# Dropping the softmax division from a differential attention block: the sum's square enters the norm's epsilon

## Chip, cores and metric

The kernel runs on one core of one Trainium2 chip. The metric is the device time of one execution in microseconds. Before the change it is 756.2 us, the median of 3 runs (755.72 to 756.58).

## The reference

One transformer block over 512 rows of width 2048: an RMS norm, a projection to six groups of 1024 columns (q, k, v, gate of the attention, pool input, gate of the pool), differential attention with 8 heads, a pooling branch, and an output projection added to x. What matters here is the attention and the norm behind it:

```python
s = einsum(q, k) * scale                      # two maps (c = 0, 1) for each head
p = softmax(s, axis=-1)
a = p[:, :, 0] - lam * p[:, :, 1]
o = einsum(a, v)                              # 2 * 64 columns a head
o = o * rsqrt(mean(o * o) + EPS) * subln_w * (1.0 - lam_init)
```

The norm's mean runs over the 128 columns of a head. With E0 and E1 for the exponentials and S0, S1 for their sums over the keys, a = E0 / S0 - lam * E1 / S1.

## The kernel before, in words

All products of TensorE are made of three: each fp32 operand is split into a high part (`w_hi`, `h_hi`, `at_hi`, cast to fp32r) and a low part (`w_lo`, `h_lo`, `at_lo`, the rest), and high times high, low times high and high times low are added in PSUM. The work has four stages. First v is projected (32 half tiles), then k of the first round. Then come four rounds (`ROUNDS`), of two heads each. Last come seven passes of the output projection (`out_half`), a scheme of seven half-sized products that take the place of eight.

A round has 40 steps, `for m in range(8, 48)`, written out by hand on every engine. In step m TensorE multiplies one half tile of weights, 512 columns, for the groups Q, U, GA, GP and K (of the next round; in the last round the first halves of the output projection). ScalarE casts the half tile of step m + 3 (`split_high`, L705) and VectorE subtracts to get its low part (`split_low`, which is `split_rest`, L923). ScalarE's cast waits on `w_used`, until TensorE has freed the buffer; VectorE's subtraction waits for the cast. Between these stands all other work of the round, each piece tied to a step.

Attention is done in eight items a round, two heads by four blocks of 128 query rows. For item i, counted from 0:

- TensorE computes both score maps in step 22 + 2i.
- VectorE takes the row maxima in step 23 + 2i (L1075), ScalarE the two exponentials in step 24 + 2i with their row sums in `row_sum` (L801).
- In step 24 + 2i VectorE forms 1/S0 and 1/S1 (`row_inv`, L1089), `coef` = -lam * S0 / S1 (L1090) and `at_raw` = E0 + coef * E1 (L1094).
- In step 25 + 2i ScalarE multiplies `at_raw` by 1/S0 (L825), and VectorE transposes it in 32x32 blocks (L1085), behind a wait for that scaling.
- SyncE moves the blocks with four DMAs (L383). In step 28 + 2i ScalarE casts `at_hi` (L808) and GpSimd subtracts to get `at_lo` (L474).

A head's product with v is run by TensorE at the end of steps 35 and 43. Behind it: ScalarE squares (`head_out`, L723, in steps 39 and 44), VectorE adds the squares over the partitions (the fold, L1107 to L1114, in steps 40 and 45), ScalarE takes the logarithm and the exponential (`log_exp`, L717 and L719, in steps 42 and 46, with `eps_t` as bias), and VectorE applies it and the gate (L1162 to L1168, in steps 43 and 47). TensorE's product of the second head in step 43 waits for `head_normed` of the first, since both use one bank.

In step 37 VectorE makes the low parts of the pool's operands (L1144, L1147). In step 40 it evacuates the group GP (`scale_evac`, L946), and TensorE waits for that before its first product of group K in the same step. In the last round VectorE also makes low parts of the output projection's forms (`form_low`, L950, in steps 38 to 41), and `mix_pool` (L996) stands in step 41, where ScalarE's `form_high(0, 3)` waits for it ahead of the next weight cast.

The order of work within a step on VectorE is: the reciprocal to at_raw, then `split_low`, then the fold, then the evacuations and the window sums, then the low parts of the pool, then the head's norm. The evacuation of GP stands at the head of step 40.

Of the kernel before, what the change touches and what calls it, by code (L numbers as in the profile page):

```python
# [9 lines left out]
ALU = mybir.AluOpType  # L10
ACT = mybir.ActivationFunctionType
AX_X = mybir.AxisListType.X

P = 128
HEAD_DIM = 64
N_WINDOWS = 4
EPS = 1e-6
# [6 lines left out]
def hybrid_block(nc, x, x_cols, norm_w, w_in, q_norm_w, k_norm_w, lq1, lk1, lq2, lk2, subln_w, w_pool,  # L24
# [10 lines left out]
    SEQ, D = x.shape  # L35
    KT = D // P
    ST = SEQ // P
# [14 lines left out]
    ITEMS = 2 * ST  # L52
# [7 lines left out]
    with ExitStack() as ctx:  # L60
        def sb(name, shape, dt=F32):
            return ctx.enter_context(nc.sbuf_tensor(name, shape, dt))

        def sem(name):
            return ctx.enter_context(nc.semaphore(name))
# [7 lines left out]
        def fixed(name, shape, dt=F32, at=None):  # L73
            offset = place[0] if at is None else at
            size = 4
            for n in shape[1:]:
                size *= n
            if at is None:
                place[0] += size
            return nc.alloc_sbuf_tensor_at(name, shape, dt, offset=offset), offset  # L80
# [27 lines left out]
        at_raw, _ = fixed("at_raw", [P, ST + 2, SEQ], at=at_lo_at)  # L108
# [23 lines left out]
        eps_t = sb("eps_t", [P, 1])  # L132
# [4 lines left out]
        neg_lam = sb("neg_lam", [P, 1])  # L137
# [1 line left out]
        x_rms = sb("x_rms", [P, ST])  # L139
        x_rstd = sb("x_rstd", [P, ST])  # L140
        neg_max = sb("neg_max", [P, 2])
        row_sum = sb("row_sum", [P, 2])
        row_inv = sb("row_inv", [P, 2])
        coef = sb("coef", [P, 1])
        neg_scaled = sb("neg_scaled", [P, 2])
# [9 lines left out]
        h_part = sb("h_part", [P, SEQ // 32])  # L155
        h_shift = sb("h_shift", [P, SEQ // 32])
        h_half = sb("h_half", [P, SEQ // 32])
        h_sums = sb("h_sums", [P, SEQ // 32])
        h_rstd = sb("h_rstd", [P, SEQ // 32])
# [81 lines left out]
        evacuated = sem("evacuated")  # L241
        v_hi_ready, v_lo_ready, pool_placed = sem("v_hi_ready"), sem("v_lo_ready"), sem("pool_placed")
        scored, max_ready, exp_done = sem("scored"), sem("max_ready"), sem("exp_done")
        at_mixed, at_scaled = sem("at_mixed"), sem("at_scaled")
        at_turned, at_hi_ready, at_lo_ready = sem("at_turned"), sem("at_hi_ready"), sem("at_lo_ready")
        at_moved = [sem(f"at_moved{n}") for n in range(2)]
        head_done, head_normed, head_mixed = sem("head_done"), sem("head_normed"), sem("head_mixed")
# [34 lines left out]
        def item_place(i):  # L282
            return (i, i) if i < ST else ((i + 2 - ST) % ST, (i + 2 - ST) % ST + 2)
# [372 lines left out]
        def _(act):  # L656
# [58 lines left out]
            def log_exp(dst, src, width, bias, count):  # L715

                nc.scalar.activation(dst, src, ACT.Ln, bias=bias, scale=1.0 / width).then_inc(log_ready, 1)  # L717
                act.wait_ge(log_ready, count)
                nc.scalar.activation(dst, dst, ACT.Exp, scale=-0.5).then_inc(rstd_ready, 1)  # L719
# [40 lines left out]
            def act_round(r, last_round=False):  # L760
                for m in range(8, 8 + HALVES):
# [12 lines left out]
                    if m == 23:  # L774
# [3 lines left out]
                                             scale=1.0 / HEAD_DIM).then_inc(q_logged, 1)  # L778
# [9 lines left out]
                    if m in (20, 22):  # L788

                        h = (m - 20) // 2  # L790
# [4 lines left out]
                    i, odd = divmod(m - 24, 2)  # L795
                    if 0 <= i < ITEMS and not odd:

                        act.wait_ge(max_ready, r * ITEMS + i + 1)
                        h, t = i // ST, item_place(i)[0]
                        for c in range(2):  # L800
                            nc.scalar.activation(probs[:, c, :], ps[:, S0 + c, :], ACT.Exp,  # L801
                                                 bias=neg_scaled[:, c:c + 1], scale=q_rstd[:, h, t, c:c + 1],
                                                 accum_out=row_sum[:, c:c + 1]).then_inc(exp_done, 1)
                    if 2 <= i < ITEMS + 2 and not odd:

                        slot = item_place(i - 2)[1]
# [8 lines left out]
                    if m == 10:  # L815
# [2 lines left out]
                        act.dma_start(wp_raw[:, :].rearrange("p (k n) -> p k n", k=2),  # L818
                                      w_pool[:, bass.ds(r * 2, 2), :]).then_inc(wp_in, 16)
                        act.dma_start(p_scale[:, :], pool_scale[:, bass.ds(r * 2, 2)]).then_inc(scale_in, 16)  # L820
                    if 0 <= i < ITEMS and odd:

                        slot = item_place(i)[1]
                        act.wait_ge(at_mixed, r * ITEMS + i + 1)
                        nc.scalar.activation(at_raw[:, slot, :], at_raw[:, slot, :], ACT.Copy, scale=row_inv[:, 0:1]  # L825
                                             ).then_inc(at_scaled, 1)
                    if m == 35:

                        act.wait_ge(diff_ready, r + 1)
# [12 lines left out]
                    if m in (39, 44):  # L842

                        h = int(m == 44)
# [6 lines left out]
                    if m in (42, 46):  # L851

                        h = int(m == 46)
                        act.wait_ge(h_folded, r * 2 + h + 1)
                        log_exp(h_rstd[:, :], h_sums[:, :], 2 * HEAD_DIM, eps_t[:, :], r * 3 + 2 + h)
                    if last_round and m == 46:
                        act.wait_ge(head_done, ROUNDS * 2)
                        nc.scalar.copy(mixed[:, (KT - 2) * SEQ:].rearrange("p (c n) -> p c n", c=2), wk(2)
# [25 lines left out]
            with act.Fori(0, ROUNDS - 1) as r:  # L884
                act_round(r)
            act_round(ROUNDS - 1, last_round=True)

            form_high(1, KP // 2 - 1)
            for h in range(18, PASSES * P_HALVES):
                p, hj = divmod(h, P_HALVES)  # L890
# [9 lines left out]
        def _(dve):  # L900
# [53 lines left out]
            def quadrant(a):  # L954
                return slice(32 * a, 32 * a + 32)
# [7 lines left out]
            def dve_round(r, last_round=False):  # L963
                def chain(ins):
                    chained[0] += 1
                    ins.then_inc(dve_step, 1)
                    dve.wait_ge(dve_step, chained[0])
# [22 lines left out]
                def mix_pool(to):  # L990
# [4 lines left out]
                    for c in range(2):  # L995
                        nc.vector.scalar_tensor_tensor(  # L996
                            out=to(c), in0=ps[:, POOL_BANK + c, :], scalar=p_scale[:, c:c + 1], in1=wk(0)[:, c, :],
                            op0=ALU.mult, op1=ALU.mult).then_inc(pool_mixed, 1)

                for m in range(8, 8 + HALVES):  # L1000

                    if m == 40:
                        dve.wait_ge(w_used, r * HALVES + before(40))
# [68 lines left out]
                    i, odd = divmod(m - 23, 2)  # L1072
# [7 lines left out]
                        for c in range(2):  # L1080
                            q_low_part(1, c)
                    if 1 <= i <= ITEMS and not odd:
                        dve.wait_ge(at_scaled, r * ITEMS + i)
                        slot = item_place(i - 1)[1]
                        nc.vector.transpose(turned[:, slot, :], at_raw[:, slot, :]).then_inc(at_turned, 1)  # L1085
                    if 0 <= i < ITEMS and odd:

                        dve.wait_ge(exp_done, r * (2 * ITEMS) + 2 * i + 2)
                        chain(nc.vector.reciprocal(row_inv[:, :], row_sum[:, :]))  # L1089
                        chain(nc.vector.scalar_tensor_tensor(out=coef[:, :], in0=row_sum[:, 0:1], scalar=neg_lam[:, :],  # L1090
                                                             in1=row_inv[:, 1:2], op0=ALU.mult, op1=ALU.mult))
                        if i == ST + 2:
                            dve.wait_ge(head_done, r * 2 + 1)
                        nc.vector.scalar_tensor_tensor(out=at_raw[:, item_place(i)[1], :], in0=probs[:, 1, :],  # L1094
                                                       scalar=coef[:, :], in1=probs[:, 0, :],
                                                       op0=ALU.mult, op1=ALU.add).then_inc(at_mixed, 1)
# [6 lines left out]
                    if m in (40, 45):  # L1103

                        h = int(m == 45)
                        dve.wait_ge(squares_ready, r * 4 + 3 + h)
                        chain(nc.vector.transpose(h_turned[:, :], head_out[:, :]))  # L1107
                        chain(nc.vector.reduce_sum(h_part[:, :], h_turned[:, :].rearrange("p (b i) -> p b i", i=32), AX_X))  # L1108
                        for a in range(2):
                            chain(nc.vector.tensor_copy(h_shift[64 * a:64 * a + 64], h_part[64 - 64 * a:128 - 64 * a]))  # L1110
                        chain(nc.vector.tensor_tensor(h_half[:, :], h_part[:, :], h_shift[:, :], ALU.add))
                        for a in range(ST):
                            chain(nc.vector.tensor_copy(h_shift[quadrant(a)], h_half[quadrant(a ^ 1)]))  # L1113
                        nc.vector.tensor_tensor(h_sums[:, :], h_half[:, :], h_shift[:, :], ALU.add).then_inc(h_folded, 1)  # L1114
# [43 lines left out]
                    if m in (43, 47):  # L1158

                        h = int(m == 47)  # L1160
# [62 lines left out]
            for r in range(ROUNDS - 1):  # L1223
                dve_round(r)
            dve_round(ROUNDS - 1, last_round=True)

            def form_sum_of(to, left, right):
# [42 lines left out]
            for h in range(18, PASSES * P_HALVES):  # L1270
                p, hj = divmod(h, P_HALVES)
# [97 lines left out]
```

## Time and profile before

| | |
|---|---|
| median of 3 runs | 756.2 us (755.72 to 756.58) |
| the profiled execution | 756.1 us |
| its span, first to last instruction | 754.3 us |
| granted TensorE clock | 1.000 of full speed throughout |
| TensorE busy | 744.7 us, 99% |
| VectorE busy | 560.7 us, 74% |
| ScalarE busy | 377.9 us, 50% |
| GpSimd busy | 79.1 us, 10% |

The span and the profiled execution differ by 1.8 us, which lie around the instructions. TensorE's products are pipelined: one of 512 columns shows 0.39 us, but one starts every 0.23 us. A line of a timeline gives the start, the duration, the engine and line, the operation, and in brackets how long the engine was idle before it and on whom it waited. Round 0 runs from about 115 to 240 us, the rounds follow each other at 125 us, and the last, round 3, ends at about 619 us.

### The profile page before, as it was taken

How to read it: one execution, taken by the hardware profiler on the slowest of the kernel's cores; microseconds unless marked ns; L12 is line 12 of the kernel's file. 1: busy time of each engine (PE TensorE's matmuls, PEld its weight loads, DVE VectorE, ACT ScalarE, POOL GpSimd, SP SyncE). 2: the span in 40 equal slices, each digit the busy share in tenths (PEclk: the TensorE clock that was granted, in tenths of full speed). 3: DMA queues.
4: the chain of work that ended last, by engine and by line, in shares of the span. 5: the costliest groups of instructions: out<-in, count | busy, mean ns of one | idle time of the engine just before them, and what ended most of it. 6: DMA issues, size and time to landing. Idle time of an engine off the chain costs nothing.

```text
span 754.3 us, 9191 instructions
## 1 busy us (share of the span) xinstructions
PE 744.7 (99%) x3266; PEld 613.3 (81%) x3266; DVE 560.7 (74%) x961; ACT 377.9 (50%) x665; POOL 79.1 (10%) x79
## 2 busy tenths in 40 slices
PE   9999999999999999999999999999999899999997
PEld 7888888888878888887888888788888678888886
DVE  5543237886766898774889877588887989987895
ACT  6472232456662345664344567225466656655552
POOL 0021000001220000120000113000022103322300
PEclk9999999999999999999999999999999999999999
DMA  9873233434332354433334433234443459999983
GB/s 315 296 264 105 91 97 113 137 105 124 111 112 79 103 143 122 124 105 93 97 112 136 128 101 112 64 120 139 126 125 96 150 162 274 277 276 267 210 192 107
DMA packets 84843, 111.39 MB, mean 148 GB/s; under 512 B 7360, under 2 KB 64960, under 8 KB 84288
## 3 DMA queue, kind: packets, MB, share of 16 engines
q1 hardware_dynamic: 78640, 92.98, 39.4%
q0 software_dynamic: 4864, 16.78, 11.2%
q10 hardware_dynamic: 1296, 1.06, 0.5%
q8 instruction: 26, 0.43, 0.2%
q14 instruction: 17, 0.14, 0.1%
HBM read 94.03 MB, written 4.19 MB: 130 GB/s over the span
## 4 chain that ended last, share of the span: by engine, by line
PE 94%; DVE 4%; ACT 1%; issue 1%; DMA 0%; DVEq 0%; ACTq 0%
PE ps L502 94%; DVE w_lo L923 1%; DVE h_lo L950 1%; DMA raw<-in_w_in 0%; DVE head_out L1164 0%; DVE head_out L1162 0%; ACT w_hi L705 0%; DVE h_shift L1113 0%; DVE h_part L1108 0%; DVE work L996 0%; DVE h_turned L1107 0%; DVE turned L1085 0%; DVE neg_max L1075 0%; ACT w_hi L758 0%; DVE work L946 0%
## 5 line engine op out<-in xcount | busy, mean ns | idle before, releaser
L502 PE MATMUL ps<-h_lo,w_hi 128*128 128x512 f32 x640 | 249.1, 389 | 0.0
L502 PE MATMUL ps<-h_hi,w_hi 128*128 128x512 f32 x640 | 249.0, 389 | 0.0
L923 DVE TENSOR_TENSOR w_lo<-raw,w_hi 128x512 fp32r<-128x512 f32 x240 | 163.9, 688 | 110.3 <-ACT w_hi L695 57.0
L502 PE MATMUL ps<-h_hi,w_lo 128*128 128x512 f32 x640 | 171.1, 389 | 0.0
L705 ACT CAST w_hi<-raw 128x512 fp32r<-128x512 f32 x149 | 92.2, 621 | 135.1 <-PE ps L502 134.6
L502 PEld LDWEIGHTS ps<-h_hi,w_hi 128*128 128x128 f32 x640 | 120.2, 188 | 25.1
L502 PEld LDWEIGHTS ps<-h_lo,w_hi 128*128 128x128 f32 x640 | 120.1, 188 | 25.1
L502 PEld LDWEIGHTS ps<-h_hi,w_lo 128*128 128x128 f32 x640 | 120.1, 188 | 25.0
L502 PE MATMUL ps<-w_hi,h_hi 128*128 128x512 f32 x352 | 122.4, 392 | 3.7 <-DVE w_lo L923 2.8
L502 PE MATMUL ps<-w_hi,h_lo 128*128 128x512 f32 x352 | 121.4, 389 | 0.0
L502 PE MATMUL ps<-w_lo,h_hi 128*128 128x512 f32 x352 | 121.4, 389 | 0.0
L474 POOL TENSOR_TENSOR at_lo<-at_raw,at_hi 128x512 fp32r<-128x512 f32 x32 | 44.3, 1385 | 493.0 <-PE ps L502 447.7
L502 PEld LDWEIGHTS ps<-w_hi,h_hi 128*128 128x128 f32 x352 | 66.3, 189 | 19.2 <-issue 2.2
L502 PEld LDWEIGHTS ps<-w_lo,h_hi 128*128 128x128 f32 x352 | 66.1, 188 | 13.9
L502 PEld LDWEIGHTS ps<-w_hi,h_lo 128*128 128x128 f32 x352 | 66.1, 188 | 13.7
L801 ACT ACTIVATE probs<-ps,neg_scaled,q_rstd 128x512 f32<-128x512 f32 x64 | 49.2, 774 | 33.5 <-DVE neg_scaled L1077 33.5
L695 ACT CAST w_hi<-raw 128x512 fp32r<-128x512 f32 x43 | 26.2, 619 | 55.4 <-PE ps L502 47.5
L1075 DVE TENSOR_REDUCE neg_max<-ps 128x2 f32<-128x1024 f32 x32 | 39.1, 1223 | 17.3 <-PE ps L502 17.3
L758 ACT CAST w_hi<-raw 128x512 fp32r<-128x512 f32 x48 | 29.3, 621 | 23.0 <-PE ps L502 22.7
L1094 DVE SCALAR_TENSOR_TENSOR at_raw<-probs,coef 128x512 f32<-128x512 f32 x32 | 24.1, 752 | 8.3 <-PE ps L502 7.3
L758 ACT CAST w_hi<-tall 128x512 fp32r<-128x512 f32 x32 | 19.9, 623 | 19.1 <-PE ps L502 19.1
L758 ACT CAST w_hi<-wide_b 128x512 fp32r<-128x512 f32 x32 | 19.8, 623 | 19.0 <-PE ps L502 17.0
(152 smaller groups left out, 730.6 us busy)
## 6 DMA issues: line engine op xcount, KB each, us to landing
raw<-in_w_in SPq DMA_DIRECT2D x95, 512.0 KB, 3.7
at_raw<-turned SPq DMA_DIRECT2D x128, 64.0 KB, 2.1
raw<-in_w_out SPq DMA_DIRECT2D x12, 512.0 KB, 3.9
raw<-in_w_out POOLq DMA_DIRECT2D x12, 512.0 KB, 17.1
wide_b<-in_w_out POOLq DMA_DIRECT2D x12, 512.0 KB, 20.3
x_rows<-in_x SPq DMA_DIRECT2D x4, 1024.0 KB, 13.8
tall<-in_w_out SPq DMA_DIRECT2D x8, 512.0 KB, 12.5
tall<-in_w_out POOLq DMA_DIRECT2D x8, 512.0 KB, 23.4
```

The source lines that it names most:

```text
L474: nc.gpsimd.tensor_tensor(at_lo[:, slot, :], at_raw[:, slot, :], at_hi[:, slot, :].bitcast(F32), ALU.subtract).then_inc(at_lo_ready, 1)
L502: last = nc.tensor.matmul(dst, lhs, rhs, start=first and i == 0, stop=final and i == len(pairs) - 1, skip_group_check=True)
L695: nc.scalar.copy(w_hi[:, n % W_SLOTS, :], raw[:, unit % RAW_SLOTS, part * 512:part * 512 + 512]).then_inc(w_hi_ready, 1)
L705: nc.scalar.copy(w_hi[:, m % W_SLOTS, :], raw[:, unit % RAW_SLOTS, part * 512:part * 512 + 512]).then_inc(w_hi_ready, 1)
L758: nc.scalar.copy(w_hi[:, h % W_SLOTS, :], src).then_inc(w_hi_ready, 1)
L801: nc.scalar.activation(probs[:, c, :], ps[:, S0 + c, :], ACT.Exp, bias=neg_scaled[:, c:c + 1], scale=q_rstd[:, h, t, c:c + 1], accum_out=r ...
L923: nc.vector.tensor_tensor(w_lo[:, slot, :], src, w_hi[:, slot, :].bitcast(F32), ALU.subtract).then_inc(w_lo_ready, 1)
L950: nc.vector.tensor_tensor(form_pair(h_lo, p, pair), form_fp32(p, pair), form_pair(h_hi, p, pair).bitcast(F32), ALU.subtract).then_inc(form ...
L1075: chain(nc.vector.reduce_max(neg_max[:, :], ps[:, S0:S0 + 2, :], AX_X, negate=True))
L1094: nc.vector.scalar_tensor_tensor(out=at_raw[:, item_place(i)[1], :], in0=probs[:, 1, :], scalar=coef[:, :], in1=probs[:, 0, :], op0=ALU.mu ...
```

## The change

`at_raw` stays undivided: A = E0 - lam * (S0 / S1) * E1, which is S0 times a. The head's output is S0 times too large in each row, and its mean square S0 squared times. The norm is therefore taken with EPS * S0 * S0 in the place of EPS, which gives the same quotient. ScalarE's scaling pass and its semaphore go; the transpose waits for `at_mixed`, an operation of VectorE itself. `row_sum` now keeps the sums of all eight items. `head_eps` squares S0 of a head's four items and places 128 * EPS * S0 * S0 in the layout of the fold by four small operations; it is called at the head of steps 38 and 43 on VectorE. The fold adds it to `h_part` on the first 32 partitions, and the logarithm's bias becomes 0.

```diff
-        row_sum = sb("row_sum", [P, 2])
+        row_sum = sb("row_sum", [P, 2, ST, 2])
+        sum_squared = sb("sum_squared", [P, 2, ST])
+        h_eps = sb("h_eps", [P, 2, SEQ // 32])
...
-                                                 accum_out=row_sum[:, c:c + 1]).then_inc(exp_done, 1)
+                                                 accum_out=row_sum[:, h, t, c:c + 1]).then_inc(exp_done, 1)
...
-                    if 0 <= i < ITEMS and odd:
-
-                        slot = item_place(i)[1]
-                        act.wait_ge(at_mixed, r * ITEMS + i + 1)
-                        nc.scalar.activation(at_raw[:, slot, :], at_raw[:, slot, :], ACT.Copy, scale=row_inv[:, 0:1]
-                                             ).then_inc(at_scaled, 1)
...
-                        log_exp(h_rstd[:, :], h_sums[:, :], 2 * HEAD_DIM, eps_t[:, :], r * 3 + 2 + h)
+                        log_exp(h_rstd[:, :], h_sums[:, :], 2 * HEAD_DIM, 0.0, r * 3 + 2 + h)
...
+                def head_eps(h):
+
+                    sums = row_sum[:, h, :, 0]
+                    chain(nc.vector.tensor_tensor(sum_squared[:, h, :], sums, sums, ALU.mult))
+                    for j in range(ST):
+                        chain(nc.vector.tensor_scalar(
+                            h_eps[0:32, h, :].rearrange("p (t j) -> p t j", j=ST)[:, :, j], sum_squared[quadrant(j), h, :],
+                            2 * HEAD_DIM * EPS, None, ALU.mult))
+
                 for m in range(8, 8 + HALVES):
+
+                    if m == 38:
+                        head_eps(0)
+                    if m == 43:
+                        head_eps(1)
...
-                        dve.wait_ge(at_scaled, r * ITEMS + i)
+                        dve.wait_ge(at_mixed, r * ITEMS + i)
...
-                        chain(nc.vector.reciprocal(row_inv[:, :], row_sum[:, :]))
-                        chain(nc.vector.scalar_tensor_tensor(out=coef[:, :], in0=row_sum[:, 0:1], scalar=neg_lam[:, :],
+                        sums = row_sum[:, i // ST, item_place(i)[0], :]
+                        chain(nc.vector.reciprocal(row_inv[:, :], sums))
+                        chain(nc.vector.scalar_tensor_tensor(out=coef[:, :], in0=sums[:, 0:1], scalar=neg_lam[:, :],
...
                         chain(nc.vector.reduce_sum(h_part[:, :], h_turned[:, :].rearrange("p (b i) -> p b i", i=32), AX_X))
+                        chain(nc.vector.tensor_tensor(h_part[0:32], h_part[0:32], h_eps[0:32, h, :], ALU.add))
```

## Rows read from the trace of the kernel before

**Rows 1.** The page's busy table: us, share of the span, instructions.
```profile
PE 744.7 (99%) x3266; PEld 613.3 (81%) x3266; DVE 560.7 (74%) x961; ACT 377.9 (50%) x665; POOL 79.1 (10%) x79
```

**Rows 2.** List of TensorE's waits: line, releaser, us in total, times, longest.
```profile
PE ps L502 <- DVE w_lo L923: 2.8, 3, 1.8
```

**Rows 3.** Groups by form: count, busy us, mean ns, idle before: the scaling pass.
```profile
L825 ACT ACTIVATE at_raw<-at_raw,row_inv 128x512 f32<-128x512 f32 x32 | 23.0, 720 | 1.1 <-DVE at_raw L1094 1.1
```

**Rows 4.** Line L1090 with min/median/max in ns; the fold's four copies, round 0.
```profile
L1090 DVE SCALAR_TENSOR_TENSOR coef<-row_sum,neg_lam,row_inv x32: 218/220/1054, 160.5 to 583.7; 128x1 f32<-128x1 f32 x32
...
216.18 0.77 DVE L1113 COPY h_shift<-h_half 32x16 f32<-32x16 f32 x4
```

**Rows 5.** Timeline of VectorE, round 0, from step 38 on.
```profile
208.35 0.16 DVE L1089 RECIPROCAL row_inv<-row_sum 128x2 f32<-128x2 f32 x1
208.54 1.05 DVE L1090 SCALAR_TENSOR_TENSOR coef<-row_sum,neg_lam,row_inv 128x1 f32<-128x1 f32 x1
209.63 0.75 DVE L1094 SCALAR_TENSOR_TENSOR at_raw<-probs,coef 128x512 f32<-128x512 f32 x1
...
212.38 1.21 DVE L946 TENSOR_TENSOR work<-ps,rstd_row 128x1024 f32<-128x1024 f32 x1
...
218.44 0.69 DVE L923 TENSOR_TENSOR w_lo<-raw,w_hi 128x512 fp32r<-128x512 f32 x1 [1.28 <-ACT w_hi L705]
...
223.88 0.69 DVE L923 TENSOR_TENSOR w_lo<-raw,w_hi 128x512 fp32r<-128x512 f32 x1 [2.03 <-ACT w_hi L705]
```

**Rows 6.** Timeline of GpSimd, round 0: at_lo twice; the line's min/median/max in ns.
```profile
207.75 1.82 POOL L474 TENSOR_TENSOR at_lo<-at_raw,at_hi 128x512 fp32r<-128x512 f32 x1 [2.28 <-ACT at_hi L808]
212.21 1.41 POOL L474 TENSOR_TENSOR at_lo<-at_raw,at_hi 128x512 fp32r<-128x512 f32 x1 [2.63 <-ACT at_hi L808]
...
L474 POOL TENSOR_TENSOR at_lo<-at_raw,at_hi x32: 1287/1293/1829, 175.9 to 598.7; 128x512 fp32r<-128x512 f32 x32
```

**Rows 7.** Timeline of ScalarE, round 0, steps 39 and 40.
```profile
209.51 0.62 ACT L705 CAST w_hi<-raw 128x512 fp32r<-128x512 f32 x1 [1.32 <-PE ps L502]
210.41 0.72 ACT L825 ACTIVATE at_raw<-at_raw,row_inv 128x512 f32<-128x512 f32 x1 [0.28 <-DVE at_raw L1094]
211.04 0.58 ACT L723 ACTIVATE head_out<-ps 128x512 f32<-128x512 f32 x1
211.52 0.61 ACT L808 CAST at_hi<-at_raw 128x512 fp32r<-128x512 f32 x1
```

**Rows 8.** SyncE's issues of the seventh item, round 0; the page's time to landing.
```profile
206.14 2.48 SPq L383 DMA_DIRECT2D at_raw<-turned  x4
...
at_raw<-turned SPq DMA_DIRECT2D x128, 64.0 KB, 2.1
```

**Rows 9.** Timeline of TensorE, round 0: first product of group K; the second head's.
```profile
214.84 0.40 PE L502 MATMUL ps<-h_hi,w_hi 128*128 128x512 f32 x1
...
226.13 0.48 PE L502 MATMUL ps<-at_hi,v_all 128*128 128x512 f32 x1 [0.22 <-DVE head_out L1164]
```

**Rows 10.** Timeline of the last round: GpSimd's at_lo of the seventh item, then VectorE.
```profile
587.41 1.73 POOL L474 TENSOR_TENSOR at_lo<-at_raw,at_hi 128x512 fp32r<-128x512 f32 x1 [2.63 <-ACT at_hi L808]
...
587.90 1.79 DVE L950 TENSOR_TENSOR h_lo<-mixed,h_hi 128x512 fp32r<-128x512 f32 x1
589.61 1.21 DVE L946 TENSOR_TENSOR work<-ps,rstd_row 128x1024 f32<-128x1024 f32 x1
...
603.03 0.75 DVE L1164 SCALAR_TENSOR_TENSOR head_out<-ps,sw,head_out 128x512 f32<-128x512 f32 x1
```

**Rows 11.** Timeline of TensorE, last round: its waits and the second head.
```profile
590.88 0.50 PE L502 MATMUL ps<-w_hi,h_hi 128*128 128x512 f32 x1 [0.68 <-DVE work L946]
...
598.41 0.47 PE L502 MATMUL ps<-w_hi,h_hi 128*128 128x512 f32 x1 [1.80 <-DVE w_lo L923]
...
604.84 0.40 PE L502 MATMUL ps<-at_hi,v_all 128*128 128x512 f32 x1
...
615.06 0.50 PE L502 MATMUL ps<-w_hi,h_hi 128*128 128x512 f32 x1 [0.40 <-DVE w_lo L923]
```

More of the change, by code:

```diff
@@ L243, in hybrid_block @@
         scored, max_ready, exp_done = sem("scored"), sem("max_ready"), sem("exp_done")
-        at_mixed, at_scaled = sem("at_mixed"), sem("at_scaled")
+        at_mixed = sem("at_mixed")
         at_turned, at_hi_ready, at_lo_ready = sem("at_turned"), sem("at_hi_ready"), sem("at_lo_ready")
```

## Prediction

> **What bounds the kernel now.** I read the page's busy table first: TensorE works for 99% of the span, so the reader should ask only where the remaining microseconds lie [rows 1]. Neither the time taken from ScalarE nor the time given to VectorE is then worth its own sum; only what moves a TensorE wait counts. The list of waits shows three of them on VectorE's low parts of weights, 2.8 us together [rows 2]. The timeline places them in the last round, between 590 and 615 us [rows 11]. Rounds 0 to 2 hold one wait each, 0.22 us, before the second head's product [rows 9]. With the 0.68 us at 590.88 [rows 11] all waits behind the start come to 2.8 + 0.7 + 3 x 0.22 = 4.2 us; that is the most that any relief could return.
>
> **What is removed.** Thirty-two scaling passes on ScalarE, 32 x 0.72 = 23.0 us [rows 3]. They sit beside TensorE's work and give no time by themselves. But in steps 39 and 40 they stand before the squares and before the cast at_hi of the seventh item. In round 0 the scaling ran from 210.41, the squares from 211.04, the cast from 211.52 [rows 7]. Without it the squares follow the weight cast of 209.51, so they start at about 210.03 and at_hi at 210.52, 1.0 us earlier. Its data are there: the four transfers were issued from 206.14 over 2.48 us, the last thus at about 208.0, and one lands in 2.1 us, at about 210.1 [rows 8]. GpSimd's at_lo, which started at 212.21, is therefore ready at about 211.2. The constant bias of the logarithm is off TensorE's path and changes nothing.
>
> **What is added.** Per head five small VectorE operations (one product of the sums, four scalings by quadrant) and one addition in the fold. The trace has no such instruction; its nearest rows are the fold's copies of 32 partitions, 0.77 us for four or 0.20 us a step with the wait behind each [rows 4], and two small ones of other kinds, the reciprocal with 0.16 and coef with 0.22 [rows 4, 5]. I take 0.20 us a step, with 0.16 and 0.25 as bounds. A round gets 12 of them, 2.4 us, and the four rounds 9.6 us. Most of it is covered: the five of step 43 fall into VectorE's wait of 2.03 us before the low part at 223.88 in rounds 0 to 2, and the fold's addition of step 40 into the 1.28 us before the one at 218.44 (or, if the fold is late, it has until the logarithm) [rows 5].
>
> **Step 38 is not covered.** VectorE has worked without a pause when it gets there. The row to look at is coef: 0.22 us at its median, 1.05 us here [rows 4, 5]. GpSimd's at_lo was issued at 207.75 and shows 1.82 us where the median is 1.29: it waited for the pool's last subtraction (L1147), which ended when the reciprocal began, ran from about 208.28 to 209.57, and coef, which reads two tensors of SBUF, finished at 209.59 [rows 5, 6]. The reciprocal, with one input, ran under it in 0.16 us from 208.35. Now the first operation behind that subtraction is the product of the sums, again with two SBUF inputs. It is held instead of coef and ends at about 209.55. Four scalings then take 0.80, the reciprocal 0.19, coef 0.25, so at_raw is mixed from 210.8, where it was 209.63: **1.17 us later**. The bounds are 0.4 (nothing of the hold is paid anew) and 1.4 (0.25 a step).
>
> The Trainium skill, page SBUF — State Buffer, section "Who interferes with whom", says that a VectorE instruction with two SBUF inputs and a GpSimd instruction that reads SBUF exclude each other, and that the order of issue decides who is blocked. The trace agrees: coef is held, the reciprocal is not.
>
> **The second meeting.** This is where I expect most of the loss. GpSimd becomes ready at 211.2, while VectorE mixes at_raw (210.8 to 211.55). The precedent is the last round: GpSimd was issued at 587.41 behind a running subtraction, got through at its end, and VectorE's next one, from 587.90, took 1.79 us instead of 0.69 [rows 10]. By that precedent the subtraction w_lo of step 38 is held 1.1 us. Before, GpSimd ran under the evacuation of GP at 212.38, which reads PSUM and one SBUF tensor and was not held (1.21 us) [rows 5, 6]. So: w_lo from 211.47, the transpose from 213.18, w_lo from 213.81, the evacuation from 214.38 to 215.59; steps of 1.71, 0.63, 0.57 as in the rows. TensorE wants it at 214.84 [rows 9]. It starts 0.06 behind it, as in the last round, where the evacuation starting at 589.61 ended at 590.82 and TensorE went on at 590.88; that is 215.65, **0.81 us late**, and the refill behind a wait adds 0.09 (the first product 0.48 instead of 0.39) [rows 9, 11]. Nothing later gives it back: the wait for the head's norm hangs on a weight cast that waits for TensorE itself. Rounds 0 to 2 have the same pattern: 3 x 0.90 = **2.7 us**.
>
> **The last round.** There the evacuation is already 0.68 us late and the 1.1 us hold is paid already, so the second meeting only changes places. TensorE's wait at 590.88 grows by 1.17. The fold's addition adds 0.20 before the pool's products, on which hangs the wait of 1.80 at 598.41: 1.37 so far. In step 43 the five operations (1.0) precede the head's norm, whose last needed step ran from 603.03 to 603.78; TensorE wants it at 604.84, a margin of 1.06 less 0.14 for the hand-over, so about 0.1 with the refill appears. The second fold's addition lengthens the wait at 615.06 by 0.20 [rows 10, 11]. Sum 1.37 + 0.1 + 0.2 = **1.7 us**. Later passes show no TensorE wait, and VectorE is no later there against TensorE than before.
>
> **Sum.** 2.7 + 1.7 = 4.4 us on a profiled execution of 756.1 us (span 754.3): 760.5. It lies 0.1 under the median of 756.2, and I leave the forecast at 760.5.
>
> **Rivals.**
> A: no second meeting in rounds 0 to 2. It decides whether w_lo of step 38 starts before 211.2. The small steps would have to be 0.07 us shorter each (0.27 over four), or GpSimd ready after 212.1, as when the cast waits for its transfers. GpSimd then runs under the transpose or the evacuation; the evacuation ends at 214.8 at the latest and TensorE waits about nothing. Only the last round pays: 756.1 + 1.7 = 757.8. For it speaks that the margin (211.47 less 211.2) is only 0.27 us; against it the precedent of 587.41.
> B, not slower: the product of the sums slips past the waiting GpSimd at 208.35. Its place is this boundary, its price 0. The four scalings and the reciprocal then run under at_lo, as the reciprocal did, coef ends near 210.0 and the mixing is 0.4 late. No second meeting reaches the evacuation; the last round pays 0.4 + 0.2 + 0.2 = 0.8: 756.9 to 757.1, within the measurement. Against it: at 587.90 the waiting GpSimd won.
> The Trainium skill, the same page and section, says that a tensor_scalar can take both ports and then contend as well; by that rule the four scalings would be held and B falls back to A or the forecast. No row here shows it.
> C, faster: ScalarE's relief brings the weight casts forward. Its casts wait 1.32 us and more for TensorE to free a buffer [rows 7], so it has nothing to bring forward; the most is a part of the 4.2 us, say 754.5.
>
> **Chances.** Forecast 0.62, A 0.20, B 0.12, C 0.06. A is measured as slower or the same with even chances, since 0.2% (1.5 us) is about what a measurement of this kernel can tell from no change. So slower 0.62 + 0.10 (half of A) + 0.02 (B with steps at their upper bound) = 0.74, same 0.10 + 0.10 = 0.20, faster 0.06. The range runs from B's end, 757.0, to 762.0: small steps of 0.25 add 0.4 at each place where VectorE is late, four times. It leaves out C, half of B and the top of the forecast's case, 0.17. The forecast's own range is 759.3 to 762.0.
>
> **What would show it.** In the trace after: a product of row sums of about 1.1 us in step 38 and coef at 0.22 (else B); at_lo of the seventh item issued about 1 us earlier and a w_lo of about 1.8 us in step 38 (else A); a new TensorE wait on the evacuation, 0.8 us in each of rounds 0 to 2; the waits near 592 and 600 together about 1.4 us longer. The prediction is wrong if TensorE waits nowhere new, or if ScalarE's casts start a queue of their own.

## The result, and the profile after

The changed kernel takes 761.5 us, the median of 4 runs (761.3 to 761.76), where the kernel before takes 756.03 on the same chip. The ratio is 1.0072, with a 95% interval of 1.0059 to 1.0085: slower by 0.7%. The forecast was 760.5. The profiled execution of after took 761.3 us with a span of 759.4, that of before 756.1 with 754.3.

The first view is the list of TensorE's waits in after (releaser; us in total, times, longest). Before it held 2.8 us on w_lo [rows 2], 0.7 on the evacuation and 0.7 on the head's norm.

```profile
PE ps L504 <- DVE work L942: 4.0, 4, 1.9
PE ps L504 <- DVE w_lo L919: 3.2, 3, 2.0
PE ps L504 <- DVE head_out L1176: 1.2, 3, 0.6
```

The wait on the evacuation of GP (`work`) now comes four times instead of once. The next view shows where it comes from: the timeline of after in round 0, VectorE from step 37 on, which answers to [rows 5].

```profile
207.58 0.68 DVE L1159 TENSOR_TENSOR wp_lo<-wp_raw,wp_hi 128x512 fp32r<-128x512 f32 x1
208.18 1.25 DVE L999 TENSOR_TENSOR sum_squared<-row_sum 128x4 f32<-128x4 f32 x1
209.47 0.74 DVE L1001 TENSOR_SCALAR h_eps<-sum_squared 32x4 f32<-32x4 f32 x4
210.25 0.17 DVE L1100 RECIPROCAL row_inv<-row_sum 128x2 f32<-128x2 f32 x1
210.45 0.22 DVE L1101 SCALAR_TENSOR_TENSOR coef<-row_sum,neg_lam,row_inv 128x1 f32<-128x1 f32 x1
210.70 0.75 DVE L1105 SCALAR_TENSOR_TENSOR at_raw<-probs,coef 128x512 f32<-128x512 f32 x1
211.37 1.78 DVE L919 TENSOR_TENSOR w_lo<-raw,w_hi 128x512 fp32r<-128x512 f32 x1
...
214.27 1.21 DVE L942 TENSOR_TENSOR work<-ps,rstd_row 128x1024 f32<-128x1024 f32 x1
```

Both meetings with GpSimd are there. The product of the sums takes 1.25 us instead of 0.15, coef is back at 0.22, and the subtraction behind at_raw takes 1.78 instead of 0.69. GpSimd and ScalarE in the same stretch, which answer to [rows 6] and [rows 7]:

```profile
207.58 1.83 POOL L476 TENSOR_TENSOR at_lo<-at_raw,at_hi 128x512 fp32r<-128x512 f32 x1 [2.27 <-ACT at_hi L810]
211.05 1.55 POOL L476 TENSOR_TENSOR at_lo<-at_raw,at_hi 128x512 fp32r<-128x512 f32 x1 [1.64 <-ACT at_hi L810]
...
209.35 0.62 ACT L707 CAST w_hi<-raw 128x512 fp32r<-128x512 f32 x1 [1.32 <-PE ps L504]
209.88 0.59 ACT L725 ACTIVATE head_out<-ps 128x512 f32<-128x512 f32 x1
210.37 0.61 ACT L810 CAST at_hi<-at_raw 128x512 fp32r<-128x512 f32 x1
```

at_lo of the seventh item is issued at 211.05 instead of 212.21. TensorE's timeline, whole kernel, the rows with a wait (against [rows 9] and [rows 11]):

```profile
215.53 0.50 PE L504 MATMUL ps<-h_hi,w_hi 128*128 128x512 f32 x1 [0.70 <-DVE work L942]
227.00 0.48 PE L504 MATMUL ps<-at_hi,v_all 128*128 128x512 f32 x1 [0.29 <-DVE head_out L1176]
...
341.62 0.50 PE L504 MATMUL ps<-h_hi,w_hi 128*128 128x512 f32 x1 [0.69 <-DVE work L942]
353.10 0.48 PE L504 MATMUL ps<-at_hi,v_all 128*128 128x512 f32 x1 [0.29 <-DVE head_out L1176]
...
467.72 0.50 PE L504 MATMUL ps<-h_hi,w_hi 128*128 128x512 f32 x1 [0.69 <-DVE work L942]
479.55 0.48 PE L504 MATMUL ps<-at_hi,v_all 128*128 128x512 f32 x1 [0.64 <-DVE head_out L1176]
...
595.39 0.50 PE L504 MATMUL ps<-w_hi,h_hi 128*128 128x512 f32 x1 [1.90 <-DVE work L942]
603.12 0.47 PE L504 MATMUL ps<-w_hi,h_hi 128*128 128x512 f32 x1 [2.00 <-DVE w_lo L919]
605.35 0.50 PE L504 MATMUL ps<-w_hi,h_hi 128*128 128x512 f32 x1 [0.59 <-DVE w_lo L919]
620.13 0.50 PE L504 MATMUL ps<-w_hi,h_hi 128*128 128x512 f32 x1 [0.59 <-DVE w_lo L919]
```

To see each round by itself I use a mark: the start of the row maximum of step 37, which always waits 1.09 us for TensorE and so follows it. From the mark of one round to that of the next lies one round; from the last mark to the end of the span lies the tail (from step 37 of round 3 on). In after the marks stand at 203.91, 330.00, 456.11 and 582.57; in before at 204.07, 329.14, 454.21 and 579.27. The median is that of all runs of a kernel; rounds, tail and clock are of its one profiled execution. "Clock" says whether the granted clock of TensorE fell within the tail while TensorE still had work. Each experiment stands beside runs of the kernel before on the same chip, whose medians were 756.0 to 756.2; the ratios are against these.

| kernel | median us | rounds, us | tail, us | clock |
|---|---|---|---|---|
| before | 756.0 to 756.2 | 125.07 125.07 125.06 | 175.03 | full |
| after | 761.5 | 126.09 126.11 126.46 | 176.83 | full |
| removal only | 755.31 | 125.08 125.07 125.07 | 174.37 | full |
| additions only | 759.28 | 125.29 125.29 125.65 | 177.68 | fell |
| cast later | 758.36 | 125.14 125.13 125.49 | 177.20 | fell |
| one input | 761.13 | 126.13 126.13 126.48 | 176.81 | full |
| reciprocal first | 763.44 (one) | 125.92 125.93 126.27 | 179.22 | fell |
| code shifted | 761.38 | 126.10 126.10 126.10 | 177.58 | fell |
| first eps moved | 756.54 | 125.16 125.13 125.14 | 174.97 | full |
| both eps moved | 756.3 | 125.07 125.06 125.07 | 174.83 | full |
| both, no fold step | 755.4 | 125.07 125.07 125.07 | 174.34 | full |
| the same, again | 755.6 | 125.06 125.07 125.07 | 174.41 | full |

Between before and after the rounds differ by 1.02 + 1.04 + 1.40 = 3.46 us, the tail by 1.80, the start by -0.16: 5.10 us, the whole difference of the spans.

### The profile page after: what moved, and what is told of

The parts are those of the page before. It is cut to its first block, busy times and chain, and to the rows that moved or that the text cites. A ratio compares the mean times of both kernels' runs of the same rounds, so it can differ in the third digit from the quotient of the medians.

```text
span 759.4 us, 9215 instructions
## 1 busy us (share of the span) xinstructions
PE 745.1 (98%) x3266; PEld 612.5 (81%) x3266; DVE 572.1 (75%) x1009; ACT 357.4 (47%) x633; POOL 78.7 (10%) x79
## 4 chain that ended last, share of the span: by engine, by line
PE 89%; DVE 9%; issue 1%; ACT 1%; DMA 0%; DVEq 0%; ACTq 0%
PE ps L504 89%; DVE w_lo L919 2%; DVE turned L1095 1%; DVE neg_max L1085 1%; DVE sum_squared L999 1%; DVE work L942 1%; DVE diff L1156 1%; DVE h_lo L946 0%; DMA raw<-in_w_in 0%; DVE at_raw L1105 0%; DVE h_eps L1001 0%; DVE wp_lo L1159 0%; DVE head_out L1176 0%; DVE head_out L1174 0%; ACT w_hi L707 0%
## 5 line engine op out<-in xcount | busy, mean ns | idle before, releaser
L919 DVE TENSOR_TENSOR w_lo<-raw,w_hi 128x512 fp32r<-128x512 f32 x240 | 168.3, 706 | 103.7 <-ACT w_hi L697 57.7
```

Of the source, the lines that this page charges most:

```text
L919: nc.vector.tensor_tensor(w_lo[:, slot, :], src, w_hi[:, slot, :].bitcast(F32), ALU.subtract).then_inc(w_lo_ready, 1)
```

## Experiments

**Theory.** The loss is two meetings of VectorE and GpSimd: the added operations of step 38 are held by at_lo of the sixth item, and the relief of ScalarE brings at_lo of the seventh forward onto w_lo of step 38. Rivals: VectorE's added work costs time as such; the early cast alone does it; the longer program does it.

**Removal only.** The added operations are left out, and with them the epsilon term of the heads' norm.

```diff
-                    if m == 38:
-                        head_eps(0)
-                    if m == 43:
-                        head_eps(1)
...
-                        chain(nc.vector.tensor_tensor(h_part[0:32], h_part[0:32], h_eps[0:32, h, :], ALU.add))
```

> The changed kernel without its additions: no head_eps, no addition in the fold, so the epsilon term is left out of the heads' norm (the output lacks it). Theory (two meetings of VectorE and GpSimd, made by the added operations and by the cast that comes 1 us early): at_raw of step 38 is mixed at about 209.5 as before, at_lo of the seventh item is still issued near 211.05, but meets the transpose and not w_lo of step 38; the evacuation of GP ends near 214.0, TensorE waits for it in no round but the last. In the last round the hold of 1.1 us is partly under the transpose, so the wait near 590 shrinks by 0.4 to 0.6. About 755.5 us, 755.1 to 756.0. Rival (the early cast alone is the loss, whatever VectorE does): a w_lo of 1.8 us in step 38 and 758.5 us or more. Rival (the added work as such is the loss): 756.0, the same as before.

Measured: 755.31 us, ratio 0.9988 (0.9978 to 0.9999), so just faster than before. The rounds are those of before, the tail is 0.66 shorter. The timeline of VectorE in round 0 shows the hold on the low part of step 39 instead of that of step 38 (the expectation had at_lo meet the transpose between them):

```profile
210.23 0.69 DVE L919 TENSOR_TENSOR w_lo<-raw,w_hi 128x512 fp32r<-128x512 f32 x1
210.84 0.71 DVE L1090 STREAM_TRANSPOSE turned<-at_raw 128x512 f32<-128x512 f32 x1
211.46 1.52 DVE L919 TENSOR_TENSOR w_lo<-raw,w_hi 128x512 fp32r<-128x512 f32 x1
212.91 1.21 DVE L942 TENSOR_TENSOR work<-ps,rstd_row 128x1024 f32<-128x1024 f32 x1
```

The evacuation starts at 212.91, before at 212.38 [rows 5], and ends at 214.12; TensorE's first product behind it starts at 214.78 with no wait. So the early cast alone does no harm; the new wait on the evacuation takes both halves of the change. In the tail the transpose covers part of the hold, and the wait near 590 is gone.

**Additions only.** The kernel before with the five operations twice a round and the fold's addition, all with the factor 0, so that nothing is added to the sums.

```diff
+                    if m == 38:
+                        head_eps(0)
+                    if m == 43:
+                        head_eps(1)
...
+                            0.0, None, ALU.mult))
```

> The kernel before with the additions alone: scaling pass and its wait kept, head_eps and the fold's addition put in with the factor 0, the bias eps_t kept, so the output is that of before. Theory: the product of sums is held 1.1 us in step 38 and at_raw is 1.2 us late in every round, but the squares and at_hi stand behind the scaling, at_lo comes near 213.3 and runs under the evacuation, which ends near 214.7; so TensorE's waits in rounds 0 to 2 stay near 0, and only the last round pays, 1.6 to 1.9 us: 757.8, 757.4 to 758.3. Rival (the added work as such): all of the loss, 761.5.

Measured: 759.28 us, ratio 1.0035 (1.0025 to 1.0045), 1 us above the expectation. As expected, w_lo of step 38 is 0.68 us and at_lo comes at 213.16. But rounds 0 and 1 are 0.22 longer than before (round 2 is 0.59 longer, of which the code-shifted kernel below says more), 0.07 of it at the head's norm and the rest at the evacuation, which ends just as TensorE comes (its first product shows 0.50 us instead of 0.40). The other miss is in the tail, where TensorE's clock fell. The columns below are the stretch, its length, then busy us of PE, PEld, DVE, ACT, POOL, and last the granted clock, the DMA share and GB/s:

```profile
600.00:601.00 1.00, 0.42 (x2) 0.41 (x3) 1.00 (x3) 1.00 (x3) 0.18 (x1) 1.00 0.00 0
601.00:605.00 4.00, 4.00 (x12) 2.69 (x11) 3.83 (x10) 2.34 (x6) 1.18 (x1) 0.57 0.24 62
605.00:610.00 5.00, 5.00 (x23) 4.05 (x22) 4.38 (x7) 1.24 (x2) 0.00 (x0) 1.00 0.61 199
```

Even with both misses the additions alone are 2.2 us short of after's time.

**Cast later.** After, with the cast at_hi of the seventh item moved behind the weight cast of step 40.

```diff
-                    if 2 <= i < ITEMS + 2 and not odd:
+                    if 2 <= i < ITEMS + 2 and not odd and m != 40:
...
+                    if m == 40:
+                        slot = item_place(i - 2)[1]
+                        act.wait_ge(at_moved[i % 2], ...)
+                        nc.scalar.copy(at_hi[:, slot, :], at_raw[:, slot, :]).then_inc(at_hi_ready, 1)
```

> The changed kernel with one instruction of ScalarE moved: in step 40 the cast at_hi of the seventh item stands behind the weight cast instead of ahead of it. Nothing is left out. Theory: at_lo is issued near 213.3 instead of 211.05 and runs under the evacuation of GP; w_lo of step 38 is 0.69 us instead of 1.78, the evacuation starts 1.1 us earlier and TensorE's wait on it (0.70 in each of rounds 0 to 2) goes, with its refill: 761.5 less 3 x 0.9 = 758.8, 758.3 to 759.3; the last round is as in the changed kernel. Rival (VectorE's added work as such, or the fetching of more code): no change, 761.5.

Measured: 758.36 us, ratio 1.0024 (1.0015 to 1.0034). VectorE and GpSimd in round 0:

```profile
207.72 1.25 DVE L1004 TENSOR_TENSOR sum_squared<-row_sum 128x4 f32<-128x4 f32 x1
...
210.90 0.68 DVE L924 TENSOR_TENSOR w_lo<-raw,w_hi 128x512 fp32r<-128x512 f32 x1
...
212.70 1.21 DVE L947 TENSOR_TENSOR work<-ps,rstd_row 128x1024 f32<-128x1024 f32 x1
...
212.83 1.29 POOL L476 TENSOR_TENSOR at_lo<-at_raw,at_hi 128x512 fp32r<-128x512 f32 x1 [3.89 <-ACT at_hi L821]
```

The first meeting is still there, the second is gone, TensorE has no wait on the evacuation in rounds 0 to 2, and each round is 0.95 to 0.98 us shorter. One instruction of ScalarE, 2.2 us later against the mark, takes back 3.1 of the 5.5 us. That settles the second meeting as the loss of rounds 0 to 2, all but 0.07 us a round and 0.36 in round 2.

**One input, and reciprocal first.** Two kernels ask what is held. In the first the product of the sums is a tensor_scalar, in the second a reciprocal; in both the epsilon term has a wrong size.

```diff
-                    chain(nc.vector.tensor_tensor(sum_squared[:, h, :], sums, sums, ALU.mult))
+                    chain(nc.vector.tensor_scalar(sum_squared[:, h, :], sums, 1.0, None, ALU.mult))
```
```diff
-                    chain(nc.vector.tensor_tensor(sum_squared[:, h, :], sums, sums, ALU.mult))
+                    chain(nc.vector.reciprocal(sum_squared[:, h, :], sums))
```

> The changed kernel with the product of the sums replaced by a tensor_scalar by 1.0 of the same size: one SBUF input instead of two, the sum is not squared, so the epsilon term has the wrong size. Theory (only instructions with two SBUF inputs are held by GpSimd here): it takes 0.16 us under at_lo, so do the four scalings, coef is held little or not; at_raw of step 38 is mixed 0.3 us late instead of 1.2, at_lo of the seventh item meets the transpose, TensorE does not wait in rounds 0 to 2: 756.6, 756.0 to 757.2. Rival (a tensor_scalar takes both ports and is held too): the first of them shows 1.1 us and more, and the time stays at 761.0 to 761.5.

> The changed kernel with the first of the five operations made a reciprocal of the same size (128x4, one SBUF input): the epsilon term has the wrong size. The run with a tensor_scalar in its place showed it held 1.1 us, while the reciprocal of 128x2 runs under at_lo in 0.16 us. If the kind decides (a reciprocal needs one port, a tensor_scalar takes two), the new first operation takes 0.16 us and the hold moves on to the first scaling, a tensor_scalar of 32x4: about 0.9 us longer than its 0.16. at_raw is then mixed 0.2 us earlier than in the changed kernel, which still meets at_lo: 760.5 to 761.5. If instead whatever stands first behind the pool's subtraction is held, the reciprocal shows 1.1 us and the scalings 0.16.

Measured: 761.13 us for the first (ratio 1.0058, 1.0038 to 1.0077), so the rival was right. The second ran once, 763.44 us, 1.9 above its range: its rounds are 0.2 us shorter than in after, as expected, but the clock fell in its tail, of which more below. By kind it answers the question. The lines give min/median/max in ns; the first is of the tensor_scalar kernel, the other two of the reciprocal kernel:

```profile
L999 DVE TENSOR_SCALAR sum_squared<-row_sum x8: 159/708/1255, 208.5 to 606.8; 128x4 f32<-128x4 f32 x8
```
```profile
L999 DVE RECIPROCAL sum_squared<-row_sum x8: 165/170/172, 208.5 to 606.0; 128x4 f32<-128x4 f32 x8
...
L1001 DVE TENSOR_SCALAR h_eps<-sum_squared x32: 158/160/1047, 208.7 to 606.8; 32x4 f32<-32x4 f32 x32
```

In step 38 a tensor_scalar with one SBUF input takes 1.25 us where it takes 0.16 in step 43. The reciprocal in its place takes 0.17 us in all eight cases, and the hold moves on to the first scaling, 1.05 us. My reading that two inputs are needed was too narrow. The Trainium skill, page SBUF — State Buffer, section "Who interferes with whom", says that a tensor_scalar can enter a mode that takes both ports and then contends with GpSimd; the two runs agree with it.

**Both eps moved, first eps moved.** The same operations where VectorE was idle: head_eps(0) in step 36 between coef and at_raw, head_eps(1) in step 44, or only the first of the two.

```diff
-                    if m == 38:
-                        head_eps(0)
-                    if m == 43:
+                    if m == 44:
                         head_eps(1)
...
                         if i == ST + 2:
+                            head_eps(0)
                             dve.wait_ge(head_done, r * 2 + 1)
```

> The changed kernel with the same operations at other places: head_eps(0) in step 36, between coef and at_raw, where VectorE waited 1.9 us for a product of TensorE; head_eps(1) at the head of step 44. Nothing is left out. Theory (the place in step 38 is the loss, the operations themselves are not): at_raw of step 38 is mixed near 209.5, at_lo of the seventh item meets the transpose, no TensorE wait on the evacuation in rounds 0 to 2; in the last round the wait near 590 is gone as in the run without the additions, and the two additions in the fold cost 0.2 us each: 755.3 + 0.4 = 755.7, 755.3 to 756.3. Rival (9.6 us more of VectorE's work must show somewhere): 758 or more.

> Only head_eps(0) is moved into step 36, head_eps(1) stays in step 43. Nothing is left out. Theory: 0.1 us more than with both moved in the last round, 0.07 us a round at the wait for the head's norm, and the 0.35 us that round 2 lost there if that belongs to the operations of step 43 and not to the place in VectorE's program: 756.1, 755.8 to 756.6. Rival: step 43 is where most of the last round's 1.8 us lies: 757 and more.

Measured: 756.3 us (ratio 1.0008, 0.9999 to 1.0017) and 756.54 us (1.0008, 0.9999 to 1.0018), both no different from before. The medians lie 0.6 and 0.4 above the expected 755.7 and 756.1. The first kernel's four runs with a mean clock of 1.000 took 755.58 to 756.17, its seven with 0.998 took 756.19 to 758.95. VectorE in step 36 of round 0, with both moved:

```profile
198.05 0.22 DVE L1099 SCALAR_TENSOR_TENSOR coef<-row_sum,neg_lam,row_inv 128x1 f32<-128x1 f32 x1
198.30 0.16 DVE L999 TENSOR_TENSOR sum_squared<-row_sum 128x4 f32<-128x4 f32 x1
198.50 0.74 DVE L1001 TENSOR_SCALAR h_eps<-sum_squared 32x4 f32<-32x4 f32 x4
200.19 0.75 DVE L1104 SCALAR_TENSOR_TENSOR at_raw<-probs,coef 128x512 f32<-128x512 f32 x1 [0.95 <-PE ps L504]
```

The five operations lie in the idle time before at_raw, which shrinks from 1.91 us in after to 0.95. All of VectorE's added work is still done, with as many instructions of VectorE (1009) as in after, and the rounds are at 125.06 to 125.07: the rivals of work as such and of the longer program fall. The second kernel tells that head_eps(1) in step 43 costs 0.07 to 0.09 us a round and 0.14 in the tail.

**Both moved, no fold step.** The epsilon rows are copied to partitions 64 to 95 as well, the other rows of h_eps are set to 0 once at the start, and the fold's first two copies become additions.

```diff
+                    chain(nc.vector.tensor_copy(h_eps[64:96, h, :], h_eps[0:32, h, :]))
...
-                        chain(nc.vector.tensor_tensor(h_part[0:32], h_part[0:32], h_eps[0:32, h, :], ALU.add))
-                            chain(nc.vector.tensor_copy(h_shift[64 * a:64 * a + 64], h_part[64 - 64 * a:128 - 64 * a]))
+                            chain(nc.vector.tensor_tensor(h_shift[64 * a:64 * a + 64], h_part[64 - 64 * a:128 - 64 * a],
+                                                          h_eps[64 - 64 * a:128 - 64 * a, h, :], ALU.add))
```

> As with both head_eps in the gaps, and no addition of its own in the fold: the epsilon rows are also copied to partitions 64 to 95 (one more small copy in each gap), and the two copies of the fold's first step become additions of the same size. Nothing is left out. Theory: the last round's two steps of 0.2 us go: 755.3, 754.9 to 755.9, the best of all. Rival (an addition of two SBUF inputs takes 0.1 us longer than the copy it replaces and eats the gain): the same as with both in the gaps.

> The kernel with both head_eps in VectorE's gaps and no step of its own in the fold, once more, for its interval against the kernel before: nothing is left out. Theory: 755.3 to 755.5, 0.6 us under the kernel before, ratio 0.9992. Rival: the same as before, and the first measurement was luck.

Measured: 755.4 us, ratio 0.9992 (0.9983 to 1.0001), and in the repetition 755.6 us, ratio 0.9994 (0.9985 to 1.0003). The tail is 0.49 and 0.42 us shorter than with the fold's additions, and 0.69 and 0.62 shorter than before. TensorE's wait near 590 is gone, as with both eps moved, and those at 598 and 614 are at 1.80 and 0.39, as before, and no longer at 2.01 and 0.59. Both medians lie 0.5 to 0.6 us under that of before, and both intervals just reach 1: the change with its operations placed well is level with the kernel before or a little better, no more.

**Code shifted.** Sixteen tiny memsets at VectorE's start.

```diff
+            for _ in range(16):
+                setup(nc.vector.memset(h_shift[:, 0:1], 0.0))
```

> The changed kernel with 16 tiny memsets more at VectorE's start, before its first data: its later program lies 16 instructions further on. Nothing is left out. In the changed kernel the low part of step 46 in round 2 started 0.46 us behind its cast instead of 0.1, and round 2 took 126.46 us where rounds 0 and 1 took 126.1. Theory (that belongs to the place in VectorE's program): the pause sits elsewhere or vanishes, round 2 takes 126.1 us, 761.5 less 0.35 = 761.15, 760.8 to 761.6. Rival (it belongs to the work of that step): unchanged in place and size.

Measured: 761.38 us, ratio 1.007 (1.0054 to 1.0085), within the range. All three rounds are 126.10, and TensorE waits 0.29 at the head's norm of round 2 as in rounds 0 and 1, where it waited 0.64 in after. The kernel with the first eps moved keeps the operations of step 43 and lacks the pause too. So 0.36 us of after's loss is not the price of those operations; it went when instructions ahead of them were added or moved. The median, 0.12 under after's, can't show it: three of the four runs have a mean clock of 0.998.

## Why the prediction was right

The profiled execution of after is 5.2 us longer than that of before, where the forecast had 4.4: 0.8 more in the rounds, 0.1 more in the tail, 0.2 less in the start, and rounding. After's median lies another 0.2 above its profiled execution.

**What bounds.** Right: the 23 us taken from ScalarE gave nothing by themselves, and the waits of TensorE hold the loss.

**Step 38.** Forecast: at_raw mixed 1.17 us late. Measured: 210.70 against 209.63, with a start 0.16 earlier, so 1.23 late. The held product, the four scalings at 0.19 a step, the reciprocal and coef are as forecast.

**The second meeting.** Forecast: at_lo ready at 211.2, w_lo held 1.1, TensorE 0.81 late behind the evacuation and 0.90 a round. Measured: issued at 211.05, w_lo 1.78 us, the evacuation wanted at 214.84 - 0.16 = 214.68 and the first product at 215.53, 0.85 late, and 0.95 a round by the cast-later run. The margin of 0.27 us on which rival A hung was there: GpSimd was issued 0.32 us before w_lo.

**The rest of the rounds.** Two small terms were missing, and they make up most of the 0.8 us between 2.7 and 3.46. The five operations of step 43, which I called covered by VectorE's wait, cost 0.07 us a round there: the low part behind them starts 0.11 us behind its cast. And 0.36 us in round 2 are a pause of VectorE that no term held; its cause stays open. The last 0.05 us a round is the wait on the evacuation, 0.95 instead of 0.90.

**The last round.** Forecast 1.7, measured 1.80. The wait near 590 grew from 0.68 to 1.90, that at 598 from 1.80 to 2.00, that at 615 from 0.40 to 0.59: 1.22, 0.20 and 0.19 against 1.17, 0.20 and 0.20. The 0.1 for the operations of step 43 showed as 0.14, the difference between the tails with the first and with both eps moved.

**Rival B and its rule.** B did not come, and by the runs with one input it could not have come as written: had the product of the sums slipped past, the first scaling behind it would have been held, 1.05 us in the reciprocal kernel. The prediction had the scalings run under at_lo there, because the reciprocal did. That half of B is wrong. It carried a chance, and no term of the sum hung on it. C did not come either: with the additions left out the tail gained 0.7 us, from the evacuation of the last round, and in round 0 no weight cast came forward against the mark.

**What no term held.** TensorE's clock. In after it was full in the profiled execution of 761.3 us; in the three others, 761.43 to 761.76, the mean clock was 0.996 to 0.998.

## What to carry to other kernels

Where one engine is busy 99% of the time, price an edit by the wait that it moves, and write out the order of starts on every engine around that wait, to a tenth of a microsecond. Taking work away from an engine that is idle half the time isn't neutral: what it releases comes earlier and may meet something else. Small operations cost nothing in a gap in which their engine waits for the bottleneck (here step 36), and their full price and more where it is late (here step 38).

## What the runs showed of the hardware that I had not expected

**The clock can fall behind a wait of 2 us.** The reciprocal-first kernel is VectorE's work of after within 0.2 us a round, yet its tail is 2.4 us longer than after's. Its stretches, columns as above:

```profile
595.00:600.00 5.00, 4.98 (x22) 4.12 (x23) 4.66 (x15) 3.29 (x3) 0.00 (x0) 1.00 0.75 224
600.00:605.00 5.00, 2.47 (x11) 1.39 (x9) 3.74 (x5) 4.03 (x9) 1.36 (x1) 0.92 0.32 124
605.00:610.00 5.00, 5.00 (x12) 3.93 (x13) 4.76 (x12) 1.27 (x3) 0.00 (x0) 0.50 0.64 200
610.00:625.00 15.00, 14.40 (x61) 11.42 (x60) 9.71 (x23) 7.56 (x14) 0.00 (x0) 0.97 0.33 102
```

TensorE had waited 1.71 us before 595.02, 1.98 before 602.75 and 0.55 before 604.97. From 605 to 610 it ran at 0.50 of the full clock, 1.2 instead of 2.4 GHz: 12 products in 5 us where the additions-only kernel made 23 at the full clock. Nor does it take a second wait. The cast-later kernel had waited once, 1.90 us before 592.02, and its clock fell right there, columns as above:

```profile
591.00:592.00 1.00, 0.00 (x0) 0.00 (x0) 1.00 (x2) 0.00 (x0) 0.00 (x0) 1.00 0.50 121
592.00:593.00 1.00, 0.98 (x2) 0.82 (x3) 1.00 (x2) 1.00 (x2) 0.00 (x0) 0.53 0.15 39
```

The kernel before has the same waits, only shorter (0.68, 1.80, 0.59), and its slowest runs, 758.5 to 759.3 us, have a mean clock of 0.995. Whether longer waits make a fall likelier is not shown: after and the one-input kernel have the longest waits (1.90 or 1.91, 2.00 and 0.59), and their profiled executions kept the full clock. Why some executions lose it and others don't stays open.

**A pause of VectorE, in one round only.** The low part of step 46 in round 2 began at 477.30, 0.46 us behind its cast; in rounds 0 and 1 the lag was 0.11 us. Four other kernels pause there too (additions only, cast later, one input, reciprocal first); the code-shifted kernel and those with head_eps(0) in step 36 don't. A fetch of code comes to mind, and the trace doesn't bear it out: the nearest transfer on a queue that carries instructions lies between 478.0 and 478.5 us, behind the pause, and the kernels with the first eps or both eps moved have one as well, between 475.0 and 475.5, and no pause. The cause is open.

**Small operations don't slip past GpSimd by being small.** An operation of 4 elements a partition was held as long as one of 512: 1.25 us against 1.78, each about 1.1 more than the 0.15 and 0.69 that they take alone.
